# Two-layer transformer with 16 experts: expert weights read in runs of 16 KB, placed by fours of rows, two neighbouring places filled by one transfer of 2 MB

## The reference, cut to what matters

```python
def expert_choice_ffn(xn, w_router, w_gate, w_up, w_down):      # 512 positions, 16 experts
    cap = CAPACITY_FACTOR * S // N_EXPERTS                      # 64
    aff = softmax(einsum('bsd,de->bse', xn, w_router))
    top_aff, top_idx = lax.top_k(swapaxes(aff, 1, 2), cap)
    xg = xn[bidx, top_idx]                                      # 64 gathered rows for each expert
    hid = silu(einsum('becd,edf->becf', xg, w_gate)) * einsum('becd,edf->becf', xg, w_up)
    y = einsum('becf,efd->becd', hid, w_down) * top_aff[..., None]
    return zeros((B, S, D)).at[bidx, top_idx].add(y)
```

## Time and profile before

| | us |
|---|---|
| median of three runs | 2094.88 |
| lowest and highest | 2093.45, 2095.03 |
| the profiled execution, its time | 2095.13 |
| its span (first to last instruction) | 2093.0 |
| TensorE busy in the span | 2052.3 (98%) |

### The profile page before, as it was taken

One profiled execution on the slowest core, in us unless ns is written; L12 is line 12 of the kernel. 1 busy time (PEld: TensorE's weight loads), 2 busy tenths in 40 slices (PEclk: granted clock), 3 DMA queues, 4 the chain that ended last, 5 costly groups with the idle time before them and its releaser, 6 DMA issues.

```text
span 2093.0 us, 23655 instructions
## 1 busy us (share of the span) xinstructions
PE 2052.3 (98%) x9752; PEld 1382.8 (66%) x9752; DVE 987.8 (47%) x1457; ACT 547.2 (26%) x1078; POOL 29.6 (1%) x16
## 2 busy tenths in 40 slices
PE   9999999999999999999999999999999999999998
PEld 5677565776888877786678788878754443333357
DVE  3776544556655454674476667644541101101145
ACT  4745452320001232203222435330140000000024
POOL 0121000000000000000000000000000000000000
PEclk9999999999999999999999999999999999999999
DMA  8311111322222120223221211212659999999961
GB/s 211 81 41 59 63 41 41 81 101 78 83 81 91 46 81 25 81 81 68 85 81 41 81 41 41 75 58 81 241 189 397 414 408 421 420 419 419 420 247 41
DMA packets 117978, 316.79 MB, mean 151 GB/s; under 512 B 38064, under 2 KB 46384, under 8 KB 93680
## 3 DMA queue, kind: packets, MB, share of 16 engines
q1 hardware_dynamic: 115520, 313.28, 40.3%
q10 hardware_dynamic: 2352, 2.00, 0.4%
HBM read 312.83 MB, written 2.10 MB: 150 GB/s over the span
## 4 chain that ended last, share of the span: by engine, by line
PE 88%; DVE 4%; ACT 4%; issue 2%; DMA 1%; DVEq 0%; SPq 0%; ACTq 0%
PE bank L459 37%; PE bank L473 17%; PE bank L3038 10%; PE bank L3088 5%; PE bank L2952 2%; PE bank L2974 2%; PE bank L1830 2%; PE bank L1406 1%; PE bank L1428 1%; PE bank L1456 1%; PE bank L2543 1%; DMA wide<-in_w_exp_gate 1%; PE bank L2533 1%; PE bank L2966 1%; PE bank L2958 1%
## 5 line engine op out<-in xcount | busy, mean ns | idle before, releaser
L459 PE MATMUL bank<-hT,ring 128*128 128x256 f32 x1168 | 268.7, 384 | 1.6 <-DVE gq L742 1.0
L459 PEld LDWEIGHTS bank<-hT,ring 128*128 128x128 f32 x1168 | 221.5, 192 | 37.8 <-issue 5.8
L473 PE MATMUL bank<-hT,ring 128*128 128x512 f32 (+1 forms) x416 | 187.8, 603 | 4.8 <-DMA ring<-in_l_w_in 4.8
L459 PE MATMUL bank<-l_quarter,l_quarter 128*128 128x256 f32 x672 | 155.2, 383 | 3.1 <-DVE gq L1750 2.6
L459 PEld LDWEIGHTS bank<-l_quarter,l_quarter 128*128 128x128 f32 x672 | 126.8, 191 | 23.5 <-DVE gq L1750 3.0
L473 PEld LDWEIGHTS bank<-hT,ring 128*128 128x128 f32 (+1 forms) x416 | 77.0, 190 | 96.9 <-issue 91.2
L3038 PE MATMUL bank<-wide,xg 128*64 128x512 f32 x488 | 124.7, 595 | 0.8 <-DMA wide<-in_w_exp_gate 0.8
L3038 PE MATMUL bank<-ring,xg 128*64 128x512 f32 x352 | 100.2, 594 | 0.0
L3206 DVE TENSOR_TENSOR xT<-bank,xT 128x512 f32<-128x512 f32 x32 | 22.1, 692 | 155.8 <-PE bank L2952 155.7
L3038 PEld LDWEIGHTS bank<-wide,xg 128*64 128x64 f32 x488 | 38.8, 137 | 75.0 <-issue 75.0
L459 PE MATMUL bank<-ring,hT 128*128 128x256 f32 x384 | 86.7, 381 | 0.2 <-DVE gv_hi L742 0.2
(11 more groups left out here) (573 smaller groups left out, 3354.4 us busy)
## 6 DMA issues: line engine op xcount, KB each, us to landing
wide<-in_w_exp_down SPq DMA_DIRECT2D x38, 1024.0 KB, 12.6
ring<-in_l_w_in SPq DMA_DIRECT2D x18, 2048.0 KB, 7.9
wide<-in_w_exp_gate SPq DMA_DIRECT2D x34, 1024.0 KB, 10.1
wide<-in_w_exp_up SPq DMA_DIRECT2D x27, 1024.0 KB, 12.2
ring<-in_w_exp_up SPq DMA_DIRECT2D x25, 1024.0 KB, 9.4
ring<-in_w_exp_down SPq DMA_DIRECT2D x21, 1024.0 KB, 13.7
ring<-in_w_in SPq DMA_DIRECT2D x10, 2048.0 KB, 8.2
ring<-in_w_exp_gate SPq DMA_DIRECT2D x19, 1024.0 KB, 10.9
```

Source lines behind the costliest of these rows:

```text
L459: mm = pe.matmul(self.out(n)[:, half * 256:half * 256 + 256], *halves[half][k], start=i == 0 and not job["goes_on"], stop=False, skip_grou ...
L473: mm = pe.matmul(self.out(n), *mats[i], start=i == 0, stop=i == len(mats) - 1)
```

## The change

The places, the transfers and the row order of the expert weights:

- A block is still 1 MB, but two blocks (two quarters `q` of one half and one expert) are cut from one run: partition p holds rows 4p to 4p + 3 of 512 rows, 16 KB in memory, and the two blocks are its first and last two rows. The order of blocks in a half is now expert 0 (both quarters), expert 1 (both quarters).
- Places are joined to five "fours" of 16 KB per partition (numbers 1, 3, 5, 7 and 13, the last after the embedding); each is filled by one transfer of 2 MB. Blocks in single places (`singles`) come in pairs of single places, by transfers of 1 MB or less. After the `LIMIT` of the single places no partner is left for `topmost`, and only the five fours go round: this holds from block 62 on.
- A place is handed on by the last block in it, so a four by its second quarter.
- The gathered rows and `hid` are ordered by fours: `even_first` writes each group of 512 as four runs of 128.

```diff
-        EXP = []
+        EXP, four_rows = [], {}
...
-                for q in range(4):
+                for half in range(2):
                     for e in range(2):
-                        stream.append((a[w][0, 2 * p + e, q * 256:(q + 1) * 256, :].rearrange("(p k) n -> p k n", k=2), 2, D))
-                        blocks.append(len(stream) - 1)
+                        four = a[w][0, 2 * p + e, half * 512:(half + 1) * 512, :].rearrange("(p k) n -> p k n", k=4)
+                        for q in range(2):
+                            stream.append((four[:, 2 * q:2 * q + 2, :], 2, D))
+                            blocks.append(len(stream) - 1)
+                            four_rows[len(stream) - 1] = four
...
+        fours = {n: four_at(x) for n, x in (
+            (1, at("wide_a", 8, [P, 4, D])[:, :, :]), (3, at("wide_b", 16, [P, 4, D])[:, :, :]),
+            (5, ring[WO2[0] % RING][:, 0:4 * D].rearrange("p (k n) -> p k n", k=4)),
+            (7, ring[WO2[1] % RING][:, 0:4 * D].rearrange("p (k n) -> p k n", k=4)),
+            (13, at("wide_c", 0, [P, 4, D])[:, :, :]))}
...
-        LIMIT = {9: NB + 8, 10: NB, 11: 3 * NB, 12: NB, 15: 1, 16: 16}
+        LIMIT = {LATER: NB + 8, 9: NB + 2, 10: NB, 11: 3 * NB, 12: NB, 15: 1, 16: 16}
+        FIRST = [(15, TOPMOST), (1,), (3,), (5,), (LATER, 9), (7,), (10, 11), (12, 16)]
...
-        for e in range(NB * len(EXP)):
-            n, by = waiting.pop(0)
-            while e >= LIMIT.get(n, e + 1):
-                n, by = waiting.pop(0)
+        for u in range(NB * len(EXP) // 2):
+            e = 2 * u
+            if u < len(FIRST):
+                places = [(n, None) for n in FIRST[u]]
+            else:
+                while waiting[0][0] in singles and (single_after(e + 1, 0) != 0 or single_after(e + 1, 1) is None):
+                    waiting.pop(0)
+                places = [waiting.pop(0)]
+                if places[0][0] in singles:
+                    places.append(waiting.pop(single_after(e + 1, 0)))
+            if places[0][0] in fours:
+                n, by = places[0]
...
+                whole_at[E0 + e] = (whole, four_rows[E0 + e])
+                taken_from[E0 + e] = by
+                last_of[n] = E0 + e + 1
+                waiting.append((n, E0 + e + 1))
...
-                last_tile[EXP[p][i]] = t0 + 24 * p + i + 1
+                last_tile[EXP[p][i]] = t0 + 24 * p + i // 4 * 4 + i % 2 * 2 + i // 2 % 2 + 1
...
         def even_first(x):
-            return x.rearrange("p (q r f) -> p q f r", q=2, r=2)
+            return x.rearrange("p (r f) -> p f r", r=4)
...
         def in_order(x):
-            return x.rearrange("p (q f r) -> p q f r", q=2, r=2)
+            return x.rearrange("p (f r) -> p f r", r=4)
...
-                                pair = EXP[p][8 * which + k // 2 * 2:8 * which + k // 2 * 2 + 2]
+                                pair = [EXP[p][8 * which + 4 * half + 2 * e + k // 2 % 2] for e in range(2)]
```

More of the change, by code:

```diff
@@ L302, in build, with four_at @@
[L302 to L306, removed]
-        LIMIT = {9: NB + 8, 10: NB, 11: 3 * NB, 12: NB, 15: 1, 16: 16}
+        def four_at(x):
+            return x, [[x[:, 2 * q + k, :] for k in range(2)] for q in range(2)]
@@ new lines, in build @@
+        early = [rows(at(f"wide{i}", 4 * i, [P, 2, D])) for i in range(2)]
+        fours = {n: four_at(x) for n, x in (
[3 more added lines that the diff above has]
+            (13, at("wide_c", 0, [P, 4, D])[:, :, :]))}
+        topmost = nc.alloc_sbuf_tensor_at("topmost", [P, 2, D], F32, offset=top)
@@ new lines, in build @@
+        EMB, TOPMOST, LATER = 13, 14, 0
+        singles = {LATER: early[1], 9: rows(at("once0", 44, [P, 2, D])),
+                   10: [at("once1", 50, [P, D])[:, :], at("once1", 54, [P, D])[:, :]],
+                   11: rows(at("once2", 36, [P, 2, D])), 12: rows(at("once3", 32, [P, 2, D])), TOPMOST: rows(topmost),
+                   15: [at(f"first{t}", t, [P, D])[:, :] for t in (48, 52)],
+                   16: [at(f"first{t}", t, [P, D])[:, :] for t in (56, 58)]}
+        LIMIT = {LATER: NB + 8, 9: NB + 2, 10: NB, 11: 3 * NB, 12: NB, 15: 1, 16: 16}
@@ L308, in build @@
+        FIRST = [(15, TOPMOST), (1,), (3,), (5,), (LATER, 9), (7,), (10, 11), (12, 16)]
+        EMB_TO = NB + 5
         ple_w_loaded = sem("ple_w_loaded")
         wpg_loaded = [sem(f"wpg_loaded{i}") for i in range(2)]
-        wide_at = {WPL: places[EMB]}
+        wide_at = {WPL: early[0]}
         load_sem = {WPL: (ple_w_loaded, 32)}
-        taken_from, last_place, times_of = {}, {}, {}
+        taken_from, last_of, whole_at = {}, {}, {}
+        level_of = {n: 16 if n < 5 or n >= TOPMOST else 32 if n < 9 else 96 if n == 9 else 64 for n in (*fours, *singles)}
@@ L313, in build @@
         order = list(range(E0))
-        TOPMOST = 14
-        waiting = [(n, None) for n in (15, TOPMOST, *range(EMB), 16)]
-        for e in range(NB * len(EXP)):
-            n, by = waiting.pop(0)
-            while e >= LIMIT.get(n, e + 1):
-                n, by = waiting.pop(0)
[L320 to L325, removed]
+        waiting = []
@@ new lines, in single_after @@
+        def single_after(e, i):
+            return next((n for n, x in enumerate(waiting) if n >= i and x[0] in singles and e < LIMIT.get(x[0], e + 1)), None)
+        for u in range(NB * len(EXP) // 2):
[10 more added lines that the diff above has]
+                n, by = places[0]
+                whole, halves = fours[n]
+                order.append(E0 + e)
+                level_of[n] += 16
+                for q in range(2):
+                    wide_at[E0 + e + q] = halves[q]
+                    load_sem[E0 + e + q] = (landed[n], level_of[n])
+                whole_at[E0 + e] = (whole, four_rows[E0 + e])
+                taken_from[E0 + e] = by
+                last_of[n] = E0 + e + 1
+                waiting.append((n, E0 + e + 1))
+            else:
+                for q, (n, by) in enumerate(places):
+                    j = E0 + e + q
+                    order.append(j)
+                    wide_at[j] = singles[n]
+                    whole = whole_of.get(id(singles[n]))
+                    if whole is not None:
+                        whole_at[j] = (whole, stream[j][0])
+                    level_of[n] += 16 if whole is not None else 32
+                    load_sem[j] = (landed[n], level_of[n])
+                    taken_from[j] = by
+                    last_of[n] = j
+                    waiting.append((n, j))
+            if e <= EMB_TO < e + 2:
@@ L3081, in tensor @@
                         for k, ns in [(k, (n,)) for n in range(2) for k in ks] if apart else [(k, range(2)) for k in ks]:
-                            pair = EXP[p][16 + k // 2 * 2:18 + k // 2 * 2]
+                            pair = [EXP[p][16 + 4 * half + 2 * e + k // 2 % 2] for e in range(2)]
                             if k % 2 == 0 and 0 in ns:
```

31 lines of the change are left out of this document (9 added, 22 removed).

## The result

| | before | changed |
|---|---|---|
| median, us | 2094.88 (2093.45 to 2095.03, 5 runs) | 2105.64 (2104.62 to 2106.23, 5 runs) |
| profiled execution: its time, span | 2095.13, 2093.0 | 2104.88, 2103.1 |

The five runs of the kernel before are the three above and two more. The ratio is 1.0052, 95% interval [1.0039, 1.0066]: 10.8 us slower. The direction was forecast; the size was not. I had 2099.1 and a range up to 2105.0, and the time lies 0.6 us beyond it.

A forecast was written before the change was run, and what follows sets the result against it. TensorE was taken as the bound, with DMA nearly so. Lost lead at pair 6 gave +4.0 us, issues, row order and start nothing: 2095.13 + 4.0 = 2099.1 us, range 2094.5 to 2105.

The forecast's parts named there:

- a lead eaten up: Weight loads in pair 6 and early pair 7: less lead in the places makes TensorE wait, half 44 starting 3.95 us later.
- The rate: Expert weight DMA: 16 KB packets at about 612 ns, 2.45 us per MB taken, against 2.497 before.
- The row order: Writes of `hid` and `rows_tm`, stepping by fours instead of twos: no change taken, bounds about 4 us gained to 5 lost.
- the issues: Expert weight queue: 86 transfers of 2 MB replace 172 of 1 MB, 0.33 us per issue, worth nothing.
- the start: Pairs 0 and 1: 16 blocks loaded ahead instead of 17, DMA pausing some 8 us after 1568, costed at nothing.
- the sum of the lead: Landing times of fours followed from half 35 through pair 6 to half 44: the end moves by +4.0 us.
- The 2.2 us between issue and transfer: Weight loads: a lone 1 MB lands 4.7 us after issue, 2.2 us more than its 2.5 us of transfer.
- Rival 1: Expert weight DMA: no gain in rate, waits in each middle pair, together 7.4 to 9 us, about 2103.5; chance 0.25.
- Rival 2: Wait ahead of half 42: TensorE's clock drops to half for 3.4 to 6.8 us, +5 to +6.5 us, 2101; chance 0.13.
- Rivals 3 and 4: Experts' stage: cheaper `hid` writes (2095.5), or 2 MB transfers under 2.3 us per MB (2094.9); 0.13 with other no-loss reasons.
- Rival 3: `hid` writes fall from 1058 to 692 ns, gaining 0.6 us in pairs 0 to 6: 2095.5; shares a chance of 0.13.

The follow-up runs named there:

- the new order of refills: Changed kernel with the first refills going to fours 1, 3 and 5 ahead of topmost: 2105.87 us, ratio 1.0054 against the kernel before.
- the layout alone: Kernel before with the new layout and row order, but 1 MB transfers, old block order and 17 places: 2094.00 against 2094.68 us, ratio 0.9995.
- the three losses: Kernel before with 10 MB of places, waiting for all four blocks of a half, and blocks handed on at its end: 2107.79 us, ratio 1.0062.
- an eleventh MB: Changed kernel with topmost kept in the round to the end, so 11 MB go round: 2101.85 against 2094.39 us, ratio 1.0032.
- fours filled by two transfers: Changed kernel with each four filled by two 1 MB transfers of 8 KB packets: 2107.45 against 2094.68 us, ratio 1.0057.
- two of them: Kernel before, 11 MB, with TensorE waiting for the whole half and blocks handed on by the half: 2102.09 against 2094.98 us, ratio 1.0037.
- the wait for the whole half: Kernel before with only TensorE's wait moved, all four blocks of a half needed at its start: +3.5 us, ratio 1.0014.

## Why the prediction was off

**Right.** The place of one part of the loss: a lead eaten up at the seam of pairs 6 and 7. I had waits of 1.3, 2.9 and 0.9 us ahead of halves 41, 42 and 43; they were 1.90, 2.72 and, ahead of 43, none (0.8 in the changed kernel with the new order of refills, where the clock stayed up). The rate: 614 ns was the median of the 16 KB packets, 612 the forecast. The row order, the issues and the start at nothing: shown by the layout alone and the new order of refills.

**The step that failed** is the one in the sum of the lead, "Those of half 34, freed 10.7 us earlier, have just gone through (9.8 us of transfer), so this is the last point with an empty queue", and with it that the middle pairs cost nothing. The 10.7 us came out (the places of half 34 were refilled at 1899.29, those of half 35 at 1909.96), the 9.8 us did not. The fours issued at 1899.29, 1899.66 and 1909.96, with us to landing:

```profile
wide_a<-in_w_exp_gate SPq DMA_DIRECT2D x1, 2048.0 KB, 9.6
...
wide_b<-in_w_exp_gate SPq DMA_DIRECT2D x1, 2048.0 KB, 14.2
...
ring<-in_w_exp_gate SPq DMA_DIRECT2D x1, 2048.0 KB, 9.4
```

The second landed at 1913.9, 14.6 us after the places were refilled and not 9.8, so 3.9 us were still queued at 1909.96, and the third landed 9.4 us after its issue where I had 2.2 + 4.9 = 7.1. From there the chain held: six fours later, 29.4 us on, the second four of half 40 landed at 1948.8. The 2.2 us between issue and transfer, which I charged for the next four, I had left out for these two, and 2.2 + 9.8 is already more than 10.7. I took an empty queue for a good sign, since it would prove that the transfers had kept up, and looked only at the balance of 9.8 us of transfer against the gap between halves; I never followed a middle pair. In such a pair 24 blocks need 58.8 of 59.3 us, which leaves 0.5 us for late starts, and in pair 4 two fours came 1.4 and 1.5 us late.

What it cost: pairs 3 to 5 were forecast at 0, and TensorE waited 4.2 us there; half 36 starts at 1909.76 instead of 1905.89, 3.9 us later. From half 36 to half 44 I had 3.95 us, and the shift grew by 7.0, to 10.9: 1.6 us ahead of halves 37 and 38, where I had no wait, and 5.4 for the rest (1.90 + 2.72 us of waits, 1.5 of work at a lower clock, less the 1.1 that the old wait had cost, and 0.3 in small pieces). After half 44, 0.8 us came back, which I had not counted. That leaves the 10.1 us of span.

The late starts in pair 4 can be summed in the prediction's own terms. If a transfer begins 2.2 us after its issue, and not before the one ahead has landed, then those of 1776.79, 1777.17 and 1787.5 land at 1785.0, 1789.9 and 1794.8, and half 25, whose other work is done at 1796.2, doesn't wait. They landed at 1786.3, 1791.2 and 1797.6: 1.3 us late, and another 1.5 at the third. 2.8 less the 1.4 to spare is 1.4; the wait was 1.50. How much of the lateness is the start of a transfer and how much the slow packets behind it isn't separated by any run, and why they are slow stays open.

That it is the places, and not what is in them, is shown from both sides: the three losses put into the kernel before give 13 us without the new layout, and an eleventh MB takes every wait out of the middle pairs.

**The rivals.** Rival 1 had the right picture of the middle pairs and nearly the right time, 2103.5, for a reason that was not there: the rate did gain, so that its time lies near is luck. The run with two transfers of 1 MB for a four is that rival, and it costs 12.8, not the 7.4 to 9 that I gave it: the same missing late starts. Rival 2, the clock, came true as well, though not at its price of 5 to 6.5 us in all. Around the wait ahead of half 42 (busy of PE, PEld, DVE, ACT, POOL, then the clock):

```profile
1966.00:1969.00 3.00, 0.43 (x2) 0.33 (x4) 1.25 (x2) 0.00 (x0) 0.00 (x0) 0.85 1.00 426
1969.00:1972.50 3.50, 3.50 (x12) 1.12 (x10) 0.00 (x0) 0.00 (x0) 0.00 (x0) 0.64 0.98 417
1972.50:1979.00 6.50, 6.50 (x28) 2.15 (x26) 0.00 (x0) 0.00 (x0) 0.00 (x0) 1.00 1.01 431
```

Late in 2.72 us without work the clock fell, and TensorE ran at half of it, 1.2 GHz, until 1971.5, about 3.4 us. It cost little. The changed kernel with the new order of refills has the same wait (2.71 us, up to 1969.60) without the drop:

```profile
1966.90:1969.60 2.70, 0.00 (x0) 0.03 (x1) 1.29 (x2) 0.00 (x0) 0.00 (x0) 1.00 1.01 431
1969.60:1973.10 3.50, 3.50 (x18) 1.44 (x20) 0.00 (x0) 0.00 (x0) 0.00 (x0) 1.00 0.98 417
```

There half 43 starts 9.80 us after half 42, held up by its load for 0.8 us; in the changed kernel it starts 10.36 us after it, so the drop cost 0.6 us. The Trainium skill (TensorE: Matmul & The Clock Gate, Part 1: The HAM clock gate) says that the idle engine falls to the lower clock; the trace of the changed kernel agrees at 1968 us, that of the other kernel doesn't. Rivals 3 and 4 did not come about: `hid` took 1046 ns, and the transfers 2.45 us per MB. Rival 3 was also priced too high: the 10 waits for `hid` of the earlier trace rows stand in pairs 2 to 6, so 0.6 us a pair makes 3 us, not 4.

The chances for the direction (0.6 slower) were fair; the range was too narrow above, because rival 1's upper end was worked out with the same missing term as the forecast.

No version of mine beats the kernel before by more than the noise. Its lead was just enough, it waits 0.8 us for loads in all, so a better rate has at most about 1 us to win.

## What to carry to other kernels

Where transfers and compute are balanced within a per cent, a bigger transfer is paid for in buffer: count the bytes held by blocks in use, when a buffer is handed on and how much must have landed at once, before you count the gain in rate. A queue that runs nearly empty is no proof of spare rate: with buffers handed on in bursts it pauses and lacks in turn, and each such restart had a price here, up to 1.5 us. A head start at the beginning did not mend a lead that was short at the end. And look for the loss in the stage where nothing seems to happen: a term put at nothing for the middle pairs needs one of them followed through.

## What the runs showed of the hardware

- The time of a packet stayed on its line: 94 ns for 2 KB, 316 for 8 KB (both with what lies between the packets), 614 ns for 16 KB (median of the packets; 630 with what lies between) in transfers issued by SP.
- A transfer that is issued when the queue is nearly dry does not start at full rate. In the changed kernel from 1778 to 1780 us, while the last queued transfer ends and the one issued at 1776.79 begins, the DMA engines count as 83 to 85% busy but move only 246 and 295 GB/s (in windows this short a packet counts where it starts):

```profile
1778.00:1779.00 1.00, 1.00 (x7) 0.87 (x6) 0.00 (x0) 0.00 (x0) 0.00 (x0) 1.00 0.85 246
1779.00:1780.00 1.00, 1.00 (x6) 0.90 (x5) 0.00 (x0) 0.00 (x0) 0.00 (x0) 1.00 0.83 295
```

- It is not a matter of the size of transfers or packets: with 1 MB transfers and 8 KB packets (fours filled by two transfers) 1781 to 1782 us show 85% and 213 GB/s.
- Waits of nearly one length had different ends. The clock fell in, or within 0.7 us after, a wait of 2.7 us (changed kernel), 2.7 us (fours filled by two transfers), 2.9 us (the three losses), 2.9 us (two of them), 3.0 us (the wait for the whole half) and 3.3 us (the eleventh MB); it stayed at full through waits of 2.72 and 2.71 us in the changed kernel with the new order of refills. In all of them TensorE had had no work for the length of the wait.
